# Modulation sums with ones as weights, and an expert loop that writes out one expert

## What is computed

```python
# first block, per layer l
mod = silu(c) @ ada_w[l] + ada_b[l]            # [6 * 1024]
h = rmsnorm(x, norm1_g[l]) * (1.0 + sc1) + sh1
x = x + g1 * token_mix(h, ...)
h = rmsnorm(x, norm2_g[l]) * (1.0 + sc2) + sh2
x = x + g2 * grouped_moe(h, ...)
# grouped_moe
for e in range(16):
    he = silu(t @ w_gate[e]) * (t @ w_up[e])
    y = y + combine[:, e:e + 1] * (he @ w_down[e])
# second block: m = silu(c) @ ada_w + ada_b, for two vectors (c and c_ctx) in its first layer
```

## Time and profile before

| | |
|---|---|
| median of 3 runs | 1956.35 us (1954.34 to 1958.11) |
| profiled execution | 1958.38 us |
| its span | 1956.6 us |
| mean granted clock of TensorE | 0.976 |
| TensorE matmuls busy | 1845.9 us (94%), 21084 records |
| weight loads busy | 1620.5 us (83%) |
| VectorE busy | 909.2 us (46%) |
| ScalarE busy | 371.7 us (19%) |
| moved by DMA | 466.09 MB, mean 238 GB/s |
| instruction queue of TensorE (q8) | 108 packets, 1.77 MB |

### The profile page before, as it was taken

How to read it: one execution, slowest core, us unless ns; L and a number is a source line. 1 busy time by engine, 2 the same in 40 slices (tenths; PEclk the granted TensorE clock), 3 DMA queues, 4 the chain that set the end, 5 groups by cost and what they waited for, 6 DMA issues and landing times.

```text
span 1956.6 us, 46189 instructions
## 1 busy us (share of the span) xinstructions
PE 1845.9 (94%) x21084; PEld 1620.5 (83%) x21084; DVE 909.2 (46%) x1598; ACT 371.7 (19%) x723; POOL 24.5 (1%) x24
## 2 busy tenths in 40 slices
PE   6999988999998999997889998999999989999999
PEld 4788776889997788786889997667888988878899
DVE  3877876200004758765000004675667661134265
ACT  3013242100002022232000004163211110021110
POOL 0000200000000000200000000000000000000000
PEclk8999989999999999998999999999999999999999
DMA  9994447699995672643999994211878563335330
GB/s 357 387 384 179 172 172 303 238 376 408 422 414 209 228 286 104 215 172 133 357 343 413 424 405 167 81 44 44 298 268 296 197 212 129 130 129 172 120 119 24
DMA packets 180616, 466.09 MB, mean 238 GB/s; under 512 B 5152, under 2 KB 55936, under 8 KB 172288
## 3 DMA queue, kind: packets, MB, share of 16 engines
q1 hardware_dynamic: 180192, 463.83, 63.9%
q10 hardware_dynamic: 288, 0.26, 0.0%
HBM read 463.03 MB, written 1.05 MB: 237 GB/s over the span
## 4 chain that ended last, share of the span: by engine, by line
PE 85%; DVE 9%; DMA 2%; ACT 2%; issue 2%; SPq 1%; ACTq 0%; DVEq 0%
PE pair L397 83%; DMA ring<-in_ada_w 2%; DVE AR L1575 2%; PE pair L1045 1%; DVE RST L1630 1%; DVE AR L1814 1%; ACT AR L1290 1%; DVE XH L1575 1%; SPq L288 0%; DVE AR L1824 0%; PE pair L902 0%; DVE AR L1828 0%; DVE XH L1815 0%; DVE AR L1868 0%; DVE AR L1806 0%
## 5 line engine op out<-in xcount | busy, mean ns | idle before, releaser
L397 PE MATMUL pair<-XH,ring 128*128 128x256 f32 (+1 forms) x3328 | 752.6, 387 | 19.7 <-ACT XH L1191 16.1
L397 PEld LDWEIGHTS pair<-XH,ring 128*128 128x128 f32 (+1 forms) x3328 | 630.3, 191 | 126.8 <-issue 31.9
L397 PE MATMUL pair<-AR,ring 128*64 128x88 f32 (+2 forms) x14336 | 699.7, 249 | 25.0 <-issue 20.6
L397 PEld LDWEIGHTS pair<-AR,ring 128*64 128x64 f32 (+1 forms) x14336 | 669.2, 139 | 48.6 <-issue 28.7
L2067 DVE TENSOR_TENSOR AR<-AR,pair 128x352 f32<-128x352 f32 x32 | 16.7, 521 | 411.4 <-PE pair L397 411.4
L1575 DVE SCALAR_TENSOR_TENSOR AR<-ring,CACT,AR 128x512 f32<-128x512 f32 x245 | 184.2, 752 | 8.7
L397 PE MATMUL pair<-AR 128*64 128x128 f32 (+3 forms) x1600 | 132.0, 292 | 8.3 <-ACT AR L1462 3.3
L397 PEld LDWEIGHTS pair<-AR 128*64 128x64 f32 (+3 forms) x1600 | 106.2, 146 | 18.0 <-issue 4.5
L2270 DVE SCALAR_TENSOR_TENSOR AR<-pair,VEC,AR 128x255 f32<-128x255 f32 x88 | 41.9, 476 | 96.0 <-ACT AR L1487 96.0
L1394 ACT ACTIVATE AR<-pair 128x352 f32 (+1 forms) x64 | 26.3, 464 | 309.9 <-PE pair L397 309.9
L1487 ACT ACTIVATE AR<-pair,VEC 128x256 f32<-128x256 f32 x88 | 36.5, 465 | 217.9 <-PE pair L397 217.9
(11 more groups left out here) (271 smaller groups left out, 1196.6 us busy)
## 6 DMA issues: line engine op xcount, KB each, us to landing
ring<-in_ada_w SPq DMA_DIRECT2D x48, 2048.0 KB, 13.1
ring<-in_w_gate SPq DMA_DIRECT2D x32, 2048.0 KB, 10.9
ring<-in_w_up SPq DMA_DIRECT2D x32, 2048.0 KB, 10.7
ring<-in_w_down SPq DMA_DIRECT2D x32, 2048.0 KB, 11.4
ring<-in_ffn_w_up SPq DMA_DIRECT2D x44, 1024.0 KB, 7.6
ring<-in_w_in SPq DMA_DIRECT2D x18, 2048.0 KB, 15.2
ring<-in_ffn_w_down SPq DMA_DIRECT2D x8, 2048.0 KB, 7.9
ring<-in_sc_w_in SPq DMA_DIRECT2D x6, 2048.0 KB, 8.5
```

Of the source, the lines that this page charges most:

```text
L397: return pe.matmul(o, lhsT, rhs, start=start, stop=stop, **kw)
```

## The change

- `turn_modulation`: the weights are 32 columns of ones, and a quarter of the accumulator's columns moves, 128 of them, into each of four column tiles. Every row of a tile of 32 partitions then holds the same sums, and a job fills 128 columns of PSUM in place of 4.
- `take_modulation`: VectorE waits for the take before, transposes 128x128 from PSUM in blocks of 32x32 into `TURNED`, waits for that, and adds the bias to one column in 32.
- The places of the sums in PSUM are 128 columns apart in place of 8.
- In the expert stage TensorE's program has the step of expert 1 written out, and a loop of seven passes over two experts (2 and 3 in its first pass).

```diff
--- before.py
+++ after.py
@@ -197,7 +197,8 @@
         CNT, OFF = [AR[:, 11 * 1024 + 512 + 32 * i:11 * 1024 + 544 + 32 * i] for i in range(2)]
         OFFI, CARRY = SM[:, 156:188].bitcast(I32), SM[:, 188:220]
         PLACE, WEIGHT = SM[:, 128:132], SM[:, 132:136]
-        FIRST_TURN = [q[:, a:a + 8] for q, a in ((PA, 0), (PA, 512), (PD, 512), (PD, 0))]
+        TURNED = RST[:, S:2 * S].rearrange("p (v n) -> p v n", v=2)
+        FIRST_TURN = [q[:, a:a + P] for q, a in ((PA, 0), (PA, 512), (PD, 512), (PD, 0))]
         CZ = XH[:, 7936:8192].rearrange("p (t n) -> p t n", t=KT)
         POS, ANG, KK = [AR[0:DQK, 1024 * i:1024 * i + S] for i in range(3)]
 
@@ -402,10 +403,10 @@
                     no = ADA_NO[a, l, k]
                     pe.wait_ge(s["rows_summed"], no + 1)
                     for w in range(n_vec(a, l, k)):
-                        acc = acc_of(a, l, k, w)
-                        for m in range(4):
-                            last = mm(q[:, 8 * n + 4 * w + m:8 * n + 4 * w + m + 1], acc[:, m * P:m * P + P], ones[:, 0:1],
-                                      True, True)
+                        acc = acc_of(a, l, k, w).rearrange("p (m j c) -> p j m c", m=4, j=4)
+                        o = q[:, P * (n + w):P * (n + w) + P]
+                        for j in range(4):
+                            last = mm(o[32 * j:32 * j + 32, :], ones[:, 0:32], acc[:, j, :, :], True, True)
                     done(last)
 
             def h_tile(n, t, w=0):
@@ -882,12 +883,11 @@
                     for k in range(4):
                         last = pe.transpose(PC[:, P * k:P * k + P], PLACED[k // 2][:, k % 2 * P:k % 2 * P + P], ident)
                     last.then_inc(s["st_turned"], 1)
-                    for e in range(1, 4):
-                        c_gate(m0 + 3 * e - 1, e)
-                        c_up(m0 + 3 * e, e)
-                        c_down(m0 + 3 * e + 1, e - 1)
-                    with pe.Fori(0, 6) as i:
-                        for e in (4, 5):
+                    c_gate(m0 + 2, 1)
+                    c_up(m0 + 3, 1)
+                    c_down(m0 + 4, 0)
+                    with pe.Fori(0, 7) as i:
+                        for e in (2, 3):
                             c = m0 + 3 * e - 1
                             c_gate(c, e, i)
                             c_up(c + 1, e, i)
@@ -1581,8 +1581,15 @@
 
                 multiplied(CHUNK_OF["ada", last_job])
                 b0 = V_ADAB + 48 * (2 * a + l) + 4 * k
+                if taken[0]:
+                    V.wait_ge(s["mod_taken"], taken[0])
+                taken[0] += 1
                 for v in range(n_vec(a, l, k)):
-                    ins = V.tensor_tensor(MOD[:, a, l, 4 * k:4 * k + 4, v], q[:, 4 * v:4 * v + 4], VEC[:, b0:b0 + 4], ALU.add)
+                    step(V.transpose(TURNED[:, v, :], q[:, P * v:P * v + P]))
+                settle()
+                for v in range(n_vec(a, l, k)):
+                    ins = V.tensor_tensor(MOD[:, a, l, 4 * k:4 * k + 4, v], TURNED[:, v, :].rearrange("p (m c) -> p m c", c=32)[:, :, 0],
+                                          VEC[:, b0:b0 + 4], ALU.add)
                 ins.then_inc(s["mod_taken"], 1)
 
             def sum_all(jobs):
@@ -1591,7 +1598,7 @@
 
             def take_all(jobs, q):
                 for n, job in enumerate(jobs):
-                    take_modulation(*job, q[:, 8 * n:8 * n + 8], jobs[-1])
+                    take_modulation(*job, q[:, P * n:], jobs[-1])
 
             def modulation(jobs, q):
 
@@ -1603,7 +1610,7 @@
                 else:
                     for n, job in enumerate(jobs):
                         sum_rows(*job)
-                        take_modulation(*job, q[:, 8 * n:8 * n + 8], job)
+                        take_modulation(*job, q[:, P * n:], job)
 
             def coef(a, l, k, last_job):
 
@@ -1616,7 +1623,7 @@
                 n_coef[0] += 1
                 V.wait_ge(s["coef_ready"], n_coef[0])
 
-            n_coef = [0]
+            n_coef, taken = [0], [0]
             V.wait_ge(s["cact_ready"], 1)
 
             def first_modulation():
```

## The result

| | before | after |
|---|---|---|
| median | 1955.92 us (4 runs, 1954.34 to 1958.11) | 1926.27 us (4 runs, 1925.36 to 1929.63) |
| ratio | | 0.9851, 95% interval 0.9834 to 0.9868 |
| profiled execution, span | 1958.38, 1956.6 us | 1925.36, 1923.6 us |

A forecast was written before the change was run, and what follows sets the result against it. The prediction took TensorE as the main bound, with DMA also full from 40 to 145 us. Loop -11.4 and modulation sums -7.8 gave -19.2 us, a median of 1937 us; its own range was 1932 to 1943, with rivals 1928 to 1949.

The forecast's parts named there:

- What bounds the kernel: Whole kernel: TensorE holds 85% of the chain of waits; expert-stage "issue" gaps are code arriving late behind weight packets.
- Part one, the loop: Expert stages: six chunks a layer turn from cold (first-met) to warm code, gaining 4.0 and 7.8 us, less jumps: -11.4 us.
- Part two: Modulation sums moved to the new form on TensorE, with VectorE's longer takes and a clock cost: -7.8 us together.
- A single between full tiles: One-vector modulation turns in ffn(0) and layer 1: 0.62 us in place of 0.81, 13 x 0.19 = 2.5 us saved.
- Beside narrow work: Six single jobs next to already narrow tiles: 0.3 us saved each, 1.8 us in all.
- A turn behind a wait: Layer 1's second turn, after TensorE's 2.23 us wait at 654.73 us: 0.8 us saved, as for other doubles.
- The clock: Longer TensorE waits, near 4 us at 122.82 us and longer at 654 us, bring slow matmuls: +1.5 and +0.3 us.
- What is saved ahead of 122.8 us is lost: Kernel start: transfers run at their limit there, so TensorE's savings on the first 13 jobs do not count.
- VectorE: Takes: a 0.3 us transpose makes each 0.3 to 0.4 us longer, mostly covered by TensorE; uncovered at most 17 us.
- the drain eats part two: Rival: tile-shape changes cost 0.35 us each and slower takes reach the path; part two 0 to +3, 1946 us; chance 0.17.
- the loop does nothing: Rival: gaps belong to the expert stage's first chunks whatever code runs; part one gives 0, 1948 us; chance 0.06.
- switches are free: Rival: turns between full tiles gain 0.36 us more each, 7 us in all, 1930 us; chance 0.13.

The follow-up runs named there:

- e5: Kernel after, with every weight transfer inside SyncE's expert loop moving only half of its chunk: 1915.11 us, ratio to before 0.979.
- e4: Kernel after, with SyncE holding expert transfers back until TensorE has done two chunks of the expert stage: 1936.44 us, ratio to before 0.9904.
- e1: Kernel before with only the expert loop changed, old sums and takes kept: 1942.58 us, ratio to before 0.9937.
- e3: Kernel before, its sums moving 32 columns of ones in place of one, the take reading every 32nd result: 1952.95 us, ratio to before 0.9993.
- e6: Kernel after, with one 32 x 32 matmul set between full-width features in each of ffn's 22 up chunks: 1937.26 us.
- e2: Kernel before with only the new modulation sums and takes, old loop kept: 1938.17 us, ratio to before 0.9914.
- e7: Kernel after, with the first 13 modulation jobs put back to the old one-column form and single add: 1927.47 us.
- e11: Kernel after without VectorE's transposes, the take reading sums straight from PSUM, so values land in wrong places: 1924.77 us.
- e8: Kernel after, with VectorE making each of its transposes twice: 1934.47 us.
- e10: Kernel after, with experts 1 to 5 written out ahead of a loop of five passes over the pair: 1948.63 us.

## Why the prediction was right or wrong

**What bounds the kernel**, and that a cold chunk is code held up by the weight traffic: right. e5 and e4 show it from both sides.

**Part one, the loop**: right. Forecast -11.4 us; SyncE's issue times give -11.8 before the jumps, and the loop alone measured -13.5. The bounds (-8 to -13) were just passed by the median.

**Part two**: the step that failed is the price of the turn on TensorE, and with it the clock. -7.8 us was forecast; alone it measured -17.9, on top of the loop -16.3 (1942.58 - 1926.27). By stretches between fixed points of the program, kernels with the old form (before, e1, e3) against those with the new. The stretches left out hold the expert stages, the hidden turns ahead of ffn(0) and what lies behind it:

| stretch | forecast | measured |
|---|---|---|
| start to layer 0's key rotation (150 us) | +0.9 | -2.4 |
| from there to the router | -2.6 | -2.6 |
| layer 1, first features to key rotation | -3.7 | -6.4 |
| from there to the router | -0.4 | -0.5 |
| ffn(0), ten singles | -1.9 | -3.4 |
| sum | -7.7 | -15.3 |

- *A single between full tiles* was priced 0.18 + 0.26 + 0.18 = 0.62 us and costs 0.47. Each term alone was a little dear or fair (e6: 0.29 to 0.37 for both changes where 0.36 was taken; a second job adds 0.22 where 0.26 was), and they overlap, which the sum left out. Thirteen times 0.15 is 2.0 us. A double was priced 0.88 and costs 0.69.
- *Beside narrow work*: the two singles at 703 and 711 us of before, ahead of and behind lat2 with its narrow tile, shrank by 1.1 us together, where 0.6 was taken; the one at 729 us went from 0.91 to 0.35, where 0.3 was taken. The old turn cost more there than between full tiles, which the trace of before showed and the prediction left out.
- *A turn behind a wait*: the old turn at 654.73 us took 2.01 us, and 3.27 in e1, where the table by stretch (648 to 652 us of e1) reads

```profile
648.00:652.00 4.00, 4.00 (x17) 3.72 (x18) 0.58 (x3) 0.00 (x0) 0.00 (x0) 0.52 1.05 403
```

  a granted clock of 0.52, the level of 1.2 GHz. The new turn there takes 0.57 us; it was over before the clock fell (1.00 from 642.6 to 643.3 us, 0.50 from 644 to 646). It was priced as any double, a saving of 0.82, though the earlier trace rows have its 2.15 us; it saved 1.4 to 2.7.
- *The clock*: +1.5 us was added for a wait of 4 us at 122.8 that would bring a slow clock. Neither came there: TensorE had waited 2.59 us for VectorE at 74.00, so that only 1.79 us were left at 121. The slow clock came behind that earlier wait, at a granted clock of 0.50, and its features took 15.16 us for 13.98; it lies where the transfers are the bound. Nor does it come each time: behind the same wait these features took 15.70 us in e2 and 14.00 in e4. The term was wrong in the rows of before as well: the wait of 0.88 us in the earlier trace rows already had a slow clock behind it (0.52 from 123.7 to 127 us), and the 32 feature matmuls took 8.96 us:

```profile
123.74 8.96 PE L397 MATMUL pair<-XH,ring 128*128 128x256 f32 x32
```

  They take 7.29 in after, but also 7.27 in e1 and e3, which have the old turns. So one of three profiles with the old turns has a slow clock there, the one with a wait ahead of it, and it is no price of the turn itself.
- *Ahead of 150 us*: 3.3 of the 7.6 us between forecast and measurement in the table lie in its first stretch, and the cause stays open. It varies from run to run: 146.9 to 149.7 us with the old form, 145.2 to 147.0 with the new. e7, whose first 13 jobs have the old form, takes 145.5 us, so the early turns do not make the difference.
- *What is saved ahead of 122.8 us is lost*: right (e7, 1.2 us).
- *VectorE*: right in size as far as can be told (e11, 1.5 us, within what two medians can differ by), and the transpose was taken at 0.3 and is 0.32. How thin the cover is (e8) was not seen.

The medians of e2 and of e1 against after give 1 to 2.6 us more than the table's sum; these stay open too.

**The rivals**: "the drain eats part two" and "the loop does nothing" fell; "switches are free" had the nearest time by the wrong reason. The range failed at its low end since it took the measured kinds of turn as if all were of the middle kind. Of its doubts about part two only the second rival gave time; the drain, the takes and the clock all had bounds that cost.

## What to carry to other kernels

Price a small insertion between long runs of TensorE by the period from one to the next, not by adding its parts, and read every instance of the old one: those beside narrow tiles and behind waits were dearer than the typical, and a good part of the gain beyond the forecast lay there. In code written out under heavy weight traffic each block met for the first time cost about 0.9 us here, so loop it; but count the instructions of the body, for a loop that is too long to be kept loses far more than it saves (77.5 us here). A cost that the other engine hides today is hidden by a margin: measure the margin by doubling the cost, and the cost itself by taking it away, since here the first came to 8.2 us and the second to 1.5, hardly more than nothing.

## What the runs showed of the hardware

- Code comes in packets of 16 KB, one for each chunk of 128 weight loads and 128 matmuls (24 packets more for 24 more cold chunks in e10), and does not run far ahead (e4). It is slower beside more data: a chunk of such code took 4.83 us with half of the weight traffic, about 5.6 with all of it, and 6.4 to 6.9 with three transfers started together.
- A loop of six chunks is kept between passes; one of twelve is fetched whole at every pass, 13 to 14 packets each. At 256 instructions a chunk these are some 1540 and 3080 instructions, an estimate. The Trainium skill (Runtime: NRT & Kernel Launch, Instruction fetch mechanics) holds that a taken branch whose target has left the window forces a fetch: the jumps back of the body of twelve agree (waits of 3.8 to 5.9 us for "issue"), and those of the body of six have no such wait.
- Two changes of tile shape with one matmul of 32 x 32 between them cost 0.29 us between long features and 0.37 where turns stand close; eight matmuls of 128 columns in their place 0.47. Where the feature tile ahead is itself 32 columns wide, the turn's first matmuls start before the last of the features (695.11 and 695.32 us).
- Eight weight loads of 128x128 took 0.81 us whether one column moved behind each or 32 (e3).
- A transpose of 128x128 fp32 from PSUM takes VectorE 0.32 us.
